# Gate and branch products turned to tokens-by-features in a two-layer encoder kernel, with the second half of the softmax scaling on ScalarE

## The chip, the cores and the metric

The kernel runs on one core of one Trainium2 chip. The metric is the device time of one execution, in microseconds (us). Before the change the median of three runs is 831.43 us (831.26 to 832.05).

## The reference, cut to what matters

256 tokens of width 1024 go through two layers. Everything is float32.

```python
h = rms_norm(x, norm1_g[l])
q, k, v ... = split(h @ w_in[l])            # four mixers A, B, C, D, four heads each
o_n = softmax(q k^T * scale + ...) v        # n = A..D, 256 columns each
y = einsum('bsnc,ncd->bsnd', o, w_branch[l])          # (256 x 256) @ (256 x 1024) per mixer
g = sigmoid(h @ w_gate[l] + b_gate[l])                # 256 x 4096
x = x + sum_n(g_n * y_n) @ w_o[l]
x = x + square(relu(rms_norm(x, norm2_g[l]) @ w_ff1[l])) @ w_ff2[l]
```

## The kernel before, in words

**Products.** Each weight is cut into a high part (`w_hi`, written by ScalarE, L575) and a low part (`w_lo`, raw minus high, written by VectorE, L810), each activation likewise (`act_hi`/`act_lo`, `part_hi`/`part_lo`). `split_product` (L1184 to L1193) makes one product out of three TensorE matmuls: high*high, high*low, low*high.

**Chunks.** The weights come in chunks of 1 MB or so, in the order of `CHUNKS`: 8 chunks of `w_in`, 16 of `w_gate` with the branch chunks `y` 0, 1, 2 between them, `y` 3, 4 of `w_o`, then `w_ff1` and `w_ff2` in turn. SyncE loads them in two halves into a raw ring of 2; the split parts live in a ring of 4. A chunk is split three steps before its product; ScalarE waits with it until the chunk four places earlier has been used (`w_used`). One step of the outer loop is one chunk; there are 28 steps before the `w_o` sums, and each engine walks through the same steps in its own hand-written order. The work of the four mixers (turning q and k, scores, softmax, turning the probabilities, values) is spread over these steps as `SCORES`, `SOFTMAX`, `TURN`, `VALUES`, `HEAD_OUT` and `X_AT` say; a pair of heads enters every second step. The softmax steps are the odd ones from 9 to 23.

**Gate and branch before.** A gate step takes 256 gate columns: two blocks of 128 features by 256 tokens, each 24 matmuls with the weight standing in the array and 256 tokens moving (`feature_blocks`, L1387 to L1390). ScalarE takes the result out of PSUM with the bias per partition (L696). A branch step makes four quarters of two feature blocks (`branch`, L1397 on); VectorE multiplies each by its gate (L1019, L1023) and adds it to `mix` (L1026). The branch results of the four mixers alternate between the two banks of `bank_w`, as do the gates; a product waits until the job two places earlier has been read (`bank_free`). After `y` 3, `mix` is cut into high and low parts (L748, L1005) and the `w_o` sums begin (`w_o_sums`).

**Softmax before.** VectorE finds the maxima (`maxima`), ScalarE takes the exponentials with their sums (L664), VectorE forms the reciprocals (L985) and scales both token tiles (L987), TensorE turns them (L1298).

**Order within a step before.** ScalarE: `heads_hi`, `probT_evac`, `evac((s,0))`, `exps`, `in_evac`, `split_hi` of chunk s+3, the gate of this step, `evac((s,1))`. VectorE: `maxima`, `heads_lo`, the first two quarters of a branch, `split_lo`, `normalise`, the last two quarters. TensorE: small product (s,0), chunk product, small product (s,1), scores, turned probabilities, values.

Of the kernel before, what the change touches and what calls it, by code (L numbers as in the profile page):

```python
# [18 lines left out]
ALU = mybir.AluOpType  # L19
# [3 lines left out]
P = 128  # L23
D = 1024
SEQ = 256
T = SEQ // P
# [26 lines left out]
Y_AFTER = {3 * n + 6: n for n in range(NB - 1)}  # L53
# [22 lines left out]
for _i in range(GATE_N):  # L76
    W_JOBS.append(("gate", _i, 0))
    if _i in Y_AFTER:
        W_JOBS += [("y", Y_AFTER[_i], q) for q in range(4)]
# [21 lines left out]
def pairs_at(first, s):  # L101
# [18 lines left out]
G1, G2, BG, GQ, GKV = 0, KD, 2 * KD, 2 * KD + NB * KD, 2 * KD + NB * KD + 2  # L120
NCOL = GKV + 1
VECTORS = {G1: KD, G2: KD, BG: NB * KD, GQ: 1, GQ + 1: 1, GKV: 1}
# [62 lines left out]
def trunk_kernel(nc, x, norm1_g, w_in, w_gate, b_gate, a_q_norm_g, a_k_norm_g, b_rel_bias, c_sink,  # L185
# [3 lines left out]
    with ctx:  # L189
# [44 lines left out]
        vec_all = sb("vec_all", [P, DEPTH * NCOL])  # L234
        root_row = sb("root_row", [P, SEQ])
# [35 lines left out]
        first_u = [bank_w[:, 0, 0:SEQ], bank_o[:, 0:SEQ]]  # L271
        turn_banks = [bank_o[:, :], bank_x[:, :], bank_acc[:, 0, :], bank_acc[:, 1, :]]
# [42 lines left out]
        x_evac = sem("x_evac")  # L315
        gate_tanh = sem("gate_tanh")
        scored = sem("scored")
        top_ready = sem("top_ready")
        exp_ready = sem("exp_ready")
        prob_ready = sem("prob_ready")  # L320
        prob_turned = sem("prob_turned")
# [6 lines left out]
        mixed = sem("mixed")  # L328
        mix_hi_ready = sem("mix_hi_ready")
# [35 lines left out]
        def split_view(buf, c):  # L365
            return buf[:, c % RING, 0:chunk_cols(c)]

# [38 lines left out]
        def _(sp):  # L406
# [3 lines left out]
            def load_half(c, h, l, g=0):  # L410
# [6 lines left out]
                if kind in ("in", "gate", "f1"):  # L417
                    w, n = {"in": (w_in, IN_C), "gate": (w_gate, 256), "f1": (w_ff1, 256)}[kind]
# [41 lines left out]
        def _(pool):  # L460
# [38 lines left out]

            def bias_run(l, r):  # L500
# [7 lines left out]
            for l in range(DEPTH):  # L508
                norm(2 * l, l)
                uq = d_w_uq[bass.ds(l, 1)].rearrange("o k n -> (o k) n")  # L510
# [35 lines left out]

                norm(2 * l + 1, l)
# [6 lines left out]
        def _(act):  # L554
# [112 lines left out]

            def probT_evac(i, l):
# [48 lines left out]
            for l in range(DEPTH):  # L717
# [11 lines left out]
                for s in range(STEPS):  # L729
# [16 lines left out]
                for q in range(4):  # L746
                    act.wait_ge(mixed, l * 12 + (8 + q + 1))
                    nc.scalar.activation(act_hi[:, 2 * q:2 * q + 2, :].rearrange("p k s -> p (k s)"), mix[:, q, :],  # L748
                                         ACT.Copy, scale=0.5).then_inc(mix_hi_ready, 1)
                split_hi(POS["o", 3], l)  # L750
                k = 2 * l + 1
# [36 lines left out]
        def _(dve):  # L788
# [190 lines left out]
            def normalise(i, l):  # L979
# [5 lines left out]
                chained(nc.vector.reciprocal(rsum[:, b, :], psum_p[:, b, :]), l)  # L985
# [15 lines left out]
            def mix_lo(q, l):  # L1001

                dve.wait_ge(mix_hi_ready, l * 4 + (q + 1))
                v = [a[:, 2 * q:2 * q + 2, :].rearrange("p k s -> p (k s)") for a in (act_hi, act_lo)]
                nc.vector.scalar_tensor_tensor(out=v[1], in0=mix[:, q, :], scalar=0.5, in1=f32(v[0]), op0=ALU.mult,  # L1005
                                               op1=ALU.subtract).then_inc(mix_lo_ready, 1)

            def branch(n, l, quarters):

                dve.wait_ge(gate_tanh, l * GATE_N + (4 * n + 4))  # L1010
                for q in quarters:
# [5 lines left out]
                    g = big[:, (4 * n + q) % 8, :]  # L1017
# [37 lines left out]
            for a, b, by in ((0, BG, 1.0), (BG, GQ, 0.5), (GQ, NCOL, 1.0)):  # L1055
                cols = slice(DEPTH * a, DEPTH * b)
                ins = nc.vector.tensor_scalar(vec_all[:, cols], bank_acc[:, 2, cols], by, None, ALU.mult)
            ins.then_inc(vec_ready, 1)
# [509 lines left out]
```

## Time and profile before

| | |
|---|---|
| median of 3 runs | 831.43 us |
| the profiled execution | 832.6 us, of which the span of the trace is 830.8 us |
| TensorE busy | 816.9 us (98%) |
| VectorE busy | 544.4 us (66%) |
| ScalarE busy | 409.6 us (49%) |
| GpSimd busy | 45.7 us (5%) |
| granted TensorE clock | 0.999 of full speed |
| DMA | 141.09 MB, mean 170 GB/s |

The busy times overlap: a core's engines run at the same time and wait for one another only through semaphores. "L1190" is line 1190 of the kernel. A row of the chain of waits gives start, length and what ran then on the path that ended last; a row of a timeline gives start, length, engine, line, operation, output<-inputs and shapes, and in brackets the idle time before it with the instruction that ended it.

### The profile page before, as it was taken

Reading aid. Unit: us, or ns where it says so; the run is one execution under the profiler, and the core shown is the slowest. Engines: PE = TensorE matmul, PEld = TensorE weight load, DVE = VectorE, ACT = ScalarE, POOL = GpSimd, SP = SyncE. Lnnn points to the kernel's source line nnn. Section 1 sums busy time; section 2 is a strip of 40 time slices with the busy share of each in tenths; the row PEclk is TensorE's granted clock in tenths of the full one; section 3 lists DMA queues with packets and bytes.
Section 4 is the critical chain, followed back from the end, with each engine's and each line's share of the span. In section 5 each row is a group of like instructions: output and inputs, shape, how many; then the busy total and the mean of one; then the engine's idle time right before and its main releaser. Section 6 shows DMA issues by size and latency. Waiting matters only on the chain.

```text
span 830.8 us, 14799 instructions
## 1 busy us (share of the span) xinstructions
PE 816.9 (98%) x5763; PEld 749.1 (90%) x5763; DVE 544.4 (66%) x805; ACT 409.6 (49%) x698; POOL 45.7 (5%) x81
## 2 busy tenths in 40 slices
PE   7999999999999999999999999999999999999996
PEld 6999979999899999999899999799988999999995
DVE  6687676865776665555767675687665865555663
ACT  6356655655454444333464475575545544333442
POOL 1420000000010000000013100000000100000000
PEclk9999999999999999999999999999999999999999
DMA  8976534536347555566546755334353665566541
GB/s 248 227 233 198 158 120 135 150 105 204 101 156 237 169 174 178 200 202 199 170 128 194 241 167 177 116 102 153 126 177 104 212 199 178 197 202 198 170 137 50
DMA packets 100851, 141.09 MB, mean 170 GB/s; under 512 B 4797, under 2 KB 87041, under 8 KB 100801
## 3 DMA queue, kind: packets, MB, share of 16 engines
q1 hardware_dynamic: 99296, 137.12, 52.1%
q0 software_dynamic: 1216, 3.17, 1.7%
q8 instruction: 34, 0.56, 0.3%
q14 instruction: 17, 0.13, 0.1%
q10 hardware_dynamic: 288, 0.11, 0.1%
HBM read 139.33 MB, written 1.05 MB: 169 GB/s over the span
## 4 chain that ended last, share of the span: by engine, by line
PE 93%; DVE 3%; ACT 1%; issue 1%; POOL 1%; DMA 1%; POOLq 0%; ACTq 0%; DVEq 0%
PE bank_w L1190 20%; PE bank_w L1192 19%; PE bank_w L1191 19%; PE bank_acc L1190 8%; PE bank_acc L1191 8%; PE bank_acc L1192 8%; PE bank_acc L1286 2%; PE bank_o L1315 2%; PE bank_acc L1298 2%; DVE w_lo L810 2%; DMA cst<-in_table 1%; PE bank_x L1263 0%; PE bank_x L1268 0%; POOL rstd L498 0%; PE bank_x L1259 0%
## 5 line engine op out<-in xcount | busy, mean ns | idle before, releaser
L810 DVE TENSOR_TENSOR w_lo<-raw,w_hi 128x1024 fp32r<-128x1024 f32 (+1 forms) x256 | 309.0, 1255 | 49.6 <-ACT w_hi L575 49.5
L1190 PE MATMUL bank_w<-act_hi,w_hi 128*128 128x256 f32 x1008 | 287.9, 286 | 0.0
L1192 PE MATMUL bank_w<-act_hi,w_lo 128*128 128x256 f32 x1008 | 285.8, 283 | 0.0
L1191 PE MATMUL bank_w<-act_lo,w_hi 128*128 128x256 f32 x1008 | 285.2, 283 | 0.0
L575 ACT ACTIVATE w_hi<-raw 128x1024 fp32r<-128x1024 f32 (+1 forms) x256 | 257.0, 1060 | 26.7 <-DMA raw<-in_w_gate 12.9
L1190 PEld LDWEIGHTS bank_w<-act_hi,w_hi 128*128 128x128 f32 x1008 | 191.6, 190 | 6.9 <-ACT big L696 3.5
L1191 PEld LDWEIGHTS bank_w<-act_lo,w_hi 128*128 128x128 f32 x1008 | 190.9, 189 | 1.8 <-issue 0.5
L1192 PEld LDWEIGHTS bank_w<-act_hi,w_lo 128*128 128x128 f32 x1008 | 191.2, 190 | 0.0
L704 ACT ACTIVATE part_hi<-big 128x512 fp32r<-128x512 f32 x32 | 20.3, 633 | 194.2 <-DVE big L1038 191.5
L1190 PE MATMUL bank_acc<-w_hi,part_hi 128*128 128x512 f32 x256 | 100.3, 392 | 0.0
L1191 PE MATMUL bank_acc<-w_lo,part_hi 128*128 128x512 f32 x256 | 100.3, 392 | 0.0
L1192 PE MATMUL bank_acc<-w_hi,part_lo 128*128 128x512 f32 x256 | 99.8, 390 | 0.0
L1038 DVE SCALAR_TENSOR_TENSOR big<-bank_w,root_row 128x512 f32<-128x512 f32 x30 | 20.7, 691 | 117.6 <-PE bank_w L1192 117.6
L1190 PE MATMUL bank_w<-w_hi,act_hi 128*128 128x268 f32 x256 | 73.9, 289 | 1.0 <-DVE act_lo L837 1.0
L1192 PE MATMUL bank_w<-w_hi,act_lo 128*128 128x268 f32 x256 | 73.2, 286 | 0.0
L1191 PE MATMUL bank_w<-w_lo,act_hi 128*128 128x268 f32 x256 | 73.2, 286 | 0.0
L696 ACT ACTIVATE big<-bank_w,vec_all 128x256 f32<-128x256 f32 x64 | 26.9, 473 | 66.0 <-PE bank_w L1192 66.0
L1192 PEld LDWEIGHTS bank_acc<-w_hi,part_lo 128*128 128x128 f32 x256 | 48.1, 188 | 10.6
L1190 PEld LDWEIGHTS bank_acc<-w_hi,part_hi 128*128 128x128 f32 x256 | 48.1, 188 | 9.5
L1191 PEld LDWEIGHTS bank_acc<-w_lo,part_hi 128*128 128x128 f32 x256 | 48.0, 188 | 8.9
L1190 PEld LDWEIGHTS bank_w<-w_hi,act_hi 128*128 128x128 f32 x256 | 48.1, 188 | 2.0 <-DVE w_lo L810 1.7
L1191 PEld LDWEIGHTS bank_w<-w_lo,act_hi 128*128 128x128 f32 x256 | 48.2, 188 | 0.0
(180 smaller groups left out, 938.5 us busy)
## 6 DMA issues: line engine op xcount, KB each, us to landing
raw<-in_w_ff SPq DMA_DIRECT2D x128, 512.0 KB, 4.7
raw<-in_w_gate SPq DMA_DIRECT2D x64, 512.0 KB, 4.7
raw<-in_w_in SPq DMA_DIRECT2D x32, 536.0 KB, 5.5
raw<-in_w_o SPq DMA_DIRECT2D x16, 512.0 KB, 4.5
raw<-in_w_branch SPq DMA_DIRECT2D x16, 256.0 KB, 4.5
raw<-in_w_branch SPq DMA_DIRECT2D x8, 512.0 KB, 4.6
xs<-in_x SPq DMA_DIRECT2D x2, 512.0 KB, 4.6
out_y<-big SPq DMA_DIRECT2D x4, 256.0 KB, 2.1
```

What stands on the lines that cost most here:

```text
L575: nc.scalar.activation(half_view(w_hi, c, h), raw_half(c, h), ACT.Copy).then_inc(w_hi_ready, 1)
L696: ins = nc.scalar.activation(big[:, i % 8, d * SEQ:(d + 1) * SEQ], bank[:, d * SEQ:(d + 1) * SEQ], ACT.Tanh, bias=vec(BG + 2 * i + d, l), ...
L704: nc.scalar.activation(part_hi[:, b, :, :].rearrange("p k s -> p (k s)"), relu[b], ACT.Square).then_inc(u_hi_ready, 1)
L810: nc.vector.tensor_tensor(half_view(w_lo, c, hf), raw_half(c, hf), f32(half_view(w_hi, c, hf)), ALU.subtract).then_inc(w_lo_ready, 1)
L1038: ins = nc.vector.scalar_tensor_tensor(out=relu[b].rearrange("p (d s) -> p d s", d=2), in0=bank_w[:, b, :].rearrange("p (d s) -> p d s", d ...
L1190: nc.tensor.matmul(dst, s_hi, m_hi, start=first, stop=False)
L1191: nc.tensor.matmul(dst, s_hi, m_lo, start=False, stop=False)
L1192: ins = nc.tensor.matmul(dst, s_lo, m_hi, start=False, stop=last)
L1286: ins = nc.tensor.matmul(bank_acc[:, half, keys], q[:, t * P:(t + 1) * P], k, start=True, stop=True)
L1298: ins = nc.tensor.transpose(bank_acc[:, 2 + b, at:at + P], prob[:, b, t, kt * P:(kt + 1) * P], ident)
L1315: ins = nc.tensor.matmul(bank_o[half * HD:(half + 1) * HD, blk * SEQ:(blk + 1) * SEQ], v, probT[:, half, kt, :], start=(kt == 0), stop=(kt ...
```

## The change

The gate and branch products are turned round: 128 tokens of the activation stand in the array and 512 weight columns move. A gate chunk is now half of the contraction (four of eight blocks of 128) for 512 columns; two chunks make a pair. In the even step of a pair both chunks are multiplied for token tile 0, in the odd step for tile 1, so that the second chunk of a pair is wanted one step earlier, and the first one is given back half-way through the second step. The gate bias now lies along the free axis: GpSimd loads it, spread over the partitions, in eight 256 KB transfers per layer, VectorE adds it while it takes the bank out of PSUM (`gate_add`), and ScalarE takes the tanh from SBUF. A gate's `gate_add` and tanh belong to the step after its product. `mix` comes out tokens by features, so each of its quarters is turned by four transposes (`turn_mix`) before it is cut for the `w_o` sums. Branch 0 moves from step 15 to 16, branch 2 from 23 to 24. VectorE scales only the first token tile of the probabilities, ScalarE the second one. On ScalarE `evac((s,1))` of a softmax step now stands ahead of the weight split, on VectorE the first two quarters of a branch stand ahead of the maxima and the last two right behind `heads_lo`. Four small products move by half a step to a step.

```diff
-Y_AFTER = {3 * n + 6: n for n in range(NB - 1)}
+Y_AFTER = {7: 0, 9: 1, 13: 2}
...
-    "lq": (11, 1), "lkv": (12, 1), "uq0": (15, 0), "uq1": (15, 1), "ukv0": (16, 0), "ukv1": (16, 1),
-    "dq0": (18, 1), "dk0": (19, 0), "dq1": (19, 1), "dk1": (20, 0),
+    "lq": (11, 1), "lkv": (12, 1), "uq0": (15, 1), "uq1": (16, 0), "ukv0": (16, 1), "ukv1": (17, 0),
+    "dq0": (18, 1), "dk0": (19, 0), "dq1": (20, 1), "dk1": (21, 1),
...
@@ SyncE
+                if kind == "gate":
+                    k = KD // 2 * (i % 2) + 2 * h
+                    src = w_gate.rearrange("l (k p) (c n) -> l c p k n", p=P, n=512)[l, i // 2]
+                    sp.dma_start(dst.rearrange("p (k n) -> p k n", k=2), src[:, k:k + 2, :]).then_inc(done, 16)
...
@@ GpSimd
+            def gate_bias(l, g):
+
+                row = b_gate[bass.ds(l, 1), g * 512:(g + 1) * 512]
+                pool.dma_start(gate_row[:, g % 2, :], row.to_broadcast([P, 512])).then_inc(gate_row_landed[g % 2], 16)
...
                 norm(2 * l, l)
+                pool.wait_ge(gate_read, l * GATE_N)
+                for g in range(2):
+                    gate_bias(l, g)
...
+                for g in range(2, GROUPS):
+                    pool.wait_ge(gate_read, l * GATE_N + 2 * (g - 1))
+                    gate_bias(l, g)
                 norm(2 * l + 1, l)
...
@@ ScalarE
-            for v, at, n in ((norm1_g, G1, KD), (norm2_g, G2, KD), (b_gate, BG, NB * KD)):
+            for v, at, n in ((norm1_g, G1, KD), (norm2_g, G2, KD)):
...
+            def normalise_second(i, l):
+
+                b = i % 2
+                act.wait_ge(rsum_ready, l * NH + (i + 1))
+                nc.scalar.activation(prob[:, b, 1, :], prob[:, b, 1, :], ACT.Copy,
+                                     scale=rsum[:, b, 1:2]).then_inc(prob_second_ready, 1)
...
-                act.wait_ge(w_used, used_count(l, POS["gate", i]))
-                if i >= 8:
-                    act.wait_ge(y_read, l * 16 + (i - 7))
-                bank = bank_w[:, W_AT["gate", i, 0] % 2, :]
-                for d in range(2):
-                    ins = nc.scalar.activation(big[:, i % 8, d * SEQ:(d + 1) * SEQ], bank[:, d * SEQ:(d + 1) * SEQ],
-                                               ACT.Tanh, bias=vec(BG + 2 * i + d, l), scale=0.5)
-                ins.then_inc(gate_tanh, 1)
+                g, t = divmod(i, 2)
+                z = gate_slot(g // 2, 2 * t + g % 2)
+                act.wait_ge(gate_read, l * GATE_N + (i + 1))
+                nc.scalar.activation(z, z, ACT.Tanh, scale=0.5).then_inc(gate_tanh, 1)
+
+            def mix_hi(q, l):
+
+                t, m = divmod(q, 2)
+                kcs = slice(m * KD // 2, (m + 1) * KD // 2)
+                act.wait_ge(mix_turned, l * 4 + (q + 1))
+                nc.scalar.activation(act_hi[:, kcs, t * P:(t + 1) * P], mix_banks[q].rearrange("p (k s) -> p k s", s=P),
+                                     ACT.Copy, scale=0.5).then_inc(mix_hi_ready, 1)
...
+                    if pair_heads(SOFTMAX, s):
+                        evac((s, 1), l)
                     for c in SPLIT_AT[s]:
                         split_hi(c, l)
-                    if kind == "gate":
-                        gate(j, l)
-                    evac((s, 1), l)
...
+                    if s > IN_N and CHUNKS[s - 1][0] == "gate":
+                        gate(CHUNKS[s - 1][1], l)
+                    if not pair_heads(SOFTMAX, s):
+                        evac((s, 1), l)
+                    for i in pair_heads(SOFTMAX, s):
+                        normalise_second(i, l)
+
+                mix_hi(0, l)
+                mix_hi(1, l)
                 split_hi(POS["o", 3], l)
+                mix_hi(2, l)
+                mix_hi(3, l)
...
@@ VectorE
-                for t in range(T):
-                    ins = nc.vector.tensor_scalar(prob[:, b, t, :], prob[:, b, t, :], rsum[:, b, t:t + 1], None, ALU.mult)
-                ins.then_inc(prob_ready, 1)
+                if i >= 2:
+                    dve.wait_ge(prob_second_ready, l * NH + (i - 1))
+                nc.vector.reciprocal(rsum[:, b, :], psum_p[:, b, :]).then_inc(rsum_ready, 1)
+                dve.wait_ge(rsum_ready, l * NH + (i + 1))
+                nc.vector.tensor_scalar(prob[:, b, 0, :], prob[:, b, 0, :], rsum[:, b, 0:1], None,
+                                        ALU.mult).then_inc(prob_ready, 1)
...
+            def gate_add(i, l):
+
+                g, t = divmod(i, 2)
+                if t == 0:
+                    dve.wait_ge(gate_row_landed[g % 2], 16 * (l * GROUPS // 2 + g // 2 + 1))
+                    dve.wait_ge(gate_first, l * GROUPS + (g + 1))
+                else:
+                    dve.wait_ge(w_used, used_count(l, POS["gate", i]))
+                nc.vector.tensor_tensor(gate_slot(g // 2, 2 * t + g % 2), bank_w[:, t, :], gate_row[:, g % 2, :],
+                                        ALU.add).then_inc(gate_read, 1)
...
+                    if s > IN_N and CHUNKS[s - 1][0] == "gate":
+                        gate_add(CHUNKS[s - 1][1], l)
+                    if kind == "y" and j < NB - 1:
+                        branch(j, l, (0, 1))
                     for i in pair_heads(SOFTMAX, s):
                         maxima(i, l)
                     for i in pair_heads(HEAD_OUT, s):
                         heads_lo(i, l)
                     if kind == "y" and j < NB - 1:
-                        branch(j, l, (0, 1))
+                        branch(j, l, (2, 3))
...
-                branch(NB - 1, l, (0,))
-                split_lo_half(POS["o", 2], 0, l)
-                branch(NB - 1, l, (1,))
+                branch(NB - 1, l, (0, 1, 2))
                 mix_lo(0, l)
-                split_lo_half(POS["o", 2], 1, l)
-                branch(NB - 1, l, (2,))
+                branch(NB - 1, l, (3,))
                 mix_lo(1, l)
-                branch(NB - 1, l, (3,))
+                split_lo(POS["o", 2], l)
+                split_lo(POS["o", 3], l)
                 mix_lo(2, l)
                 mix_lo(3, l)
-                split_lo(POS["o", 3], l)
...
@@ TensorE
+                pe.wait_ge(prob_second_ready, l * NH + (i + 1))
...
+                g, t = divmod(i, 2)
+                tok = slice(t * P, (t + 1) * P)
+                bank_free(("gate", g, t), l)
+                for half in range(2):
+                    c = POS["gate", 2 * g + half]
+                    hi, lo = k_view(w_hi, c, KD // 2), k_view(w_lo, c, KD // 2)
+                    if t == 0:
+                        pe.wait_ge(w_lo_ready, lo_count(l, c))
+                    sides = [(act_hi[:, half * KD // 2 + k, tok], act_lo[:, half * KD // 2 + k, tok], hi[:, k, :], lo[:, k, :])
+                             for k in range(KD // 2)]
+                    ins = split_product(bank_w[:, t, :], sides, half == 0, half == 1)
+                    if t == 1:
+                        ins.then_inc(w_used, 1)
...
+            def turn_mix(q, l):
+
+                pe.wait_ge(mixed, l * 12 + (8 + q + 1))
+                for j in range(KD // 2):
+                    ins = nc.tensor.transpose(mix_banks[q][:, j * P:(j + 1) * P], mix[:, q, j * P:(j + 1) * P], ident)
+                ins.then_inc(mix_turned, 1)
+
+            def last_branch(l):
+
+                for q in range(3):
+                    branch_part(NB - 1, q, l)
+                turn_mix(0, l)
+                branch_part(NB - 1, 3, l)
+                turn_mix(1, l)
...
                 for c in range(4):
-                    pe.wait_ge(mix_lo_ready, l * 4 + (c + 1))
+                    pe.wait_ge(mix_lo_ready, l * 4 + (c // 2 + 1))
...
+                    if c == 0:
+                        turn_mix(2, l)
+                        turn_mix(3, l)
+                pe.wait_ge(mix_lo_ready, l * 4 + 4)
                 part(0, 2)
```

## Rows read from the trace of the kernel before

**Rows 1.** The page: span, and busy time of each engine.
```profile
span 830.8 us, 14799 instructions
...
PE 816.9 (98%) x5763; PEld 749.1 (90%) x5763; DVE 544.4 (66%) x805; ACT 409.6 (49%) x698; POOL 45.7 (5%) x81
```

**Rows 2.** Busy time in one stretch: PE, PEld, DVE, ACT, POOL, clock, DMA.
```profile
60.00:190.00 130.00, 130.00 (x1030) 118.38 (x1029) 92.29 (x177) 78.29 (x168) 1.46 (x3) 1.00 0.47 142
```

**Rows 3.** Chain of waits around one gate product: start, us, what.
```profile
482.06 0.12 PE bank_w L1190
...
487.81 0.22 PE bank_x L1251 x2
```

**Rows 4.** Chain of waits in the MLP: 24 wide matmuls between these two.
```profile
327.22 0.24 PE bank_acc L1190
...
332.71 0.12 PE bank_w L1190
```

**Rows 5.** Groups of instructions: count, busy us, mean ns, idle before.
```profile
L810 DVE TENSOR_TENSOR w_lo<-raw,w_hi 128x1024 fp32r<-128x1024 f32 x224 | 262.2, 1219 | 48.9 <-ACT w_hi L575 48.9
...
L704 ACT ACTIVATE part_hi<-big 128x512 fp32r<-128x512 f32 x32 | 20.3, 633 | 194.2 <-DVE big L1038 191.5 <-DVE big L1035 2.7
...
L987 DVE TENSOR_SCALAR prob<-prob,rsum 128x256 f32<-128x256 f32 x64 | 19.7, 351 | 1.1
...
L1026 DVE TENSOR_TENSOR mix<-mix,tmp 128x512 f32<-128x512 f32 x24 | 16.6, 692 | 0.8
```

**Rows 6.** VectorE's timeline, steps 7 to 9 of layer 0, then step 8 of layer 1.
```profile
61.03 4.62 DVE L810 TENSOR_TENSOR w_lo<-raw,w_hi 128x1024 fp32r<-128x1024 f32 x4
...
71.50 0.48 DVE L908 COPY vd<-qkv 128x256 f32<-128x256 f32 x2
...
73.55 0.68 DVE L969 TENSOR_REDUCE top<-bank_acc 128x2 f32<-128x512 f32 x1
...
81.11 0.94 DVE L926 TENSOR_SCALAR qkv<-qkv,rs_d 128x192 f32<-128x192 f32 x4
...
478.45 0.49 DVE L908 COPY vd<-qkv 128x256 f32<-128x256 f32 x2
```

**Rows 7.** Chain of waits: layer 0's turning, small products, values; layer 1's turning.
```profile
60.63 0.44 PE bank_x L1247 x4
...
81.69 1.02 PE bank_acc L1298 x8
...
112.85 0.65 PE bank_x L1258 x2
113.50 0.84 PE bank_x L1259 x2
...
121.71 1.01 PE bank_o L1315 x8
...
468.04 0.44 PE bank_x L1247 x4
```

**Rows 8.** VectorE's timeline, layer 0, branch step 19.
```profile
146.67 0.70 DVE L967 SCALAR_TENSOR_TENSOR bank_acc<-cst,bank_acc 128x512 f32<-128x512 f32 x1 [0.90 <-PE bank_acc L1286]
...
149.73 0.69 DVE L1023 SCALAR_TENSOR_TENSOR tmp<-big,bank_w 128x512 f32<-128x512 f32 x1
```

**Rows 9.** ScalarE's timeline behind the last gate of layer 0.
```profile
205.73 0.84 ACT L696 ACTIVATE big<-bank_w,vec_all 128x256 f32<-128x256 f32 x2 [3.64 <-PE bank_w L1192]
206.46 2.01 ACT L575 ACTIVATE w_hi<-raw 128x1024 fp32r<-128x1024 f32 x2
```

**Rows 10.** Chain of waits, layer 0: the first transposes for the second norm.
```profile
226.13 0.22 PE bank_o L1201 x2
```

**Rows 11.** DMA issues: count, KB each, median us to landing.
```profile
raw<-in_w_gate SPq DMA_DIRECT2D x64, 512.0 KB, 4.7
...
w_ukv<-in_d_w_ukv POOLq DMA_DIRECT2D x2, 256.0 KB, 5.0
```

**Rows 12.** Chain of waits at the start of the kernel.
```profile
9.85 0.29 DVE vec_all L1057 x2
```

More of the change, by code:

```diff
@@ L75 @@
 W_JOBS = []
[L76 to L79, printed above, removed]
+for _g in range(GROUPS):
+    W_JOBS += [("gate", _g, t) for t in range(T)]
+    if 2 * _g + 1 in Y_AFTER:
+        W_JOBS += [("y", Y_AFTER[2 * _g + 1], q) for q in range(4)]
 W_JOBS += [("y", NB - 1, q) for q in range(4)]
@@ L315, in trunk_kernel @@
         x_evac = sem("x_evac")
+        gate_row_landed = [sem(f"gate_row_landed{b}") for b in range(2)]
+        gate_first = sem("gate_first")
+        gate_read = sem("gate_read")
         gate_tanh = sem("gate_tanh")
@@ L366, in split_view, with gate_slot @@
             return buf[:, c % RING, 0:chunk_cols(c)]
+        def gate_slot(n, q):
+            return big[:, (4 * n + q) % 8, :]
         def loads_of_half(c):
@@ L416, in load_half @@
                 dst = raw_half(c, h)
-                if kind in ("in", "gate", "f1"):
-                    w, n = {"in": (w_in, IN_C), "gate": (w_gate, 256), "f1": (w_ff1, 256)}[kind]
+                if kind == "gate":
+                    k = KD // 2 * (i % 2) + 2 * h
+                    src = w_gate.rearrange("l (k p) (c n) -> l c p k n", p=P, n=512)[l, i // 2]
+                    sp.dma_start(dst.rearrange("p (k n) -> p k n", k=2), src[:, k:k + 2, :]).then_inc(done, 16)
+                elif kind in ("in", "f1"):
+                    w, n = {"in": (w_in, IN_C), "f1": (w_ff1, 256)}[kind]
                     src = w.rearrange("l (k p) (c n) -> l c p k n", p=P, n=n)[bass.ds(l, 1), bass.ds(i + 2 * g, 1)]
@@ L1001, in mix_lo @@
             def mix_lo(q, l):
+                t, m = divmod(q, 2)
                 dve.wait_ge(mix_hi_ready, l * 4 + (q + 1))
-                v = [a[:, 2 * q:2 * q + 2, :].rearrange("p k s -> p (k s)") for a in (act_hi, act_lo)]
-                nc.vector.scalar_tensor_tensor(out=v[1], in0=mix[:, q, :], scalar=0.5, in1=f32(v[0]), op0=ALU.mult,
-                                               op1=ALU.subtract).then_inc(mix_lo_ready, 1)
+                hi, lo = (a[:, m * KD // 2:(m + 1) * KD // 2, t * P:(t + 1) * P] for a in (act_hi, act_lo))
+                nc.vector.scalar_tensor_tensor(out=lo, in0=mix_banks[q].rearrange("p (k s) -> p k s", s=P), scalar=0.5,
+                                               in1=f32(hi), op0=ALU.mult, op1=ALU.subtract).then_inc(mix_lo_ready, 1)
+            def gate_add(i, l):
[7 more added lines that the diff above has]
+                                        ALU.add).then_inc(gate_read, 1)
             def branch(n, l, quarters):
@@ L1054, in _ @@
             dve.wait_ge(rows_turned, 1)
[L1055 to L1058, printed above, removed]
+            nc.vector.tensor_copy(vec_all[:, :], bank_acc[:, 2, 0:DEPTH * NCOL]).then_inc(vec_ready, 1)
             dve.wait_ge(vec_ready, 1)
@@ L1091, in _ @@
                     if kind == "y" and j < NB - 1:
-                        branch(j, l, (2, 3))
                         for c in SPLIT_AT[s]:
@@ L1392, in gate @@
             def gate(i, l):
-                bank_free(("gate", i, 0), l)
-                pe.wait_ge(w_lo_ready, lo_count(l, POS["gate", i]))
-                feature_blocks(bank_w[:, W_AT["gate", i, 0] % 2, :], POS["gate", i])
+                g, t = divmod(i, 2)
[11 more added lines that the diff above has]
+                        ins.then_inc(w_used, 1)
@@ new lines, in gate, with branch_part @@
+                if t == 0:
+                    ins.then_inc(gate_first, 1)
+            def branch_part(n, q, l):
+                c, (t, m) = POS["y", n], divmod(q, 2)
+                tok, cols = slice(t * P, (t + 1) * P), slice(m * 512, (m + 1) * 512)
+                hi, lo = k_view(w_hi, c, 2), k_view(w_lo, c, 2)
+                if q == 0:
+                    pe.wait_ge(w_lo_ready, lo_count(l, c))
+                    pe.wait_ge(o_lo_ready, l * (NH // 2) + (2 * n + 2))
+                bank_free(("y", n, q), l)
+                sides = [(part_hi[:, n % 2, k, tok], part_lo[:, n % 2, k, tok], hi[:, k, cols], lo[:, k, cols]) for k in range(2)]
+                split_product(bank_w[:, W_AT["y", n, q] % 2, :], sides, True, True).then_inc(y_done if q < 3 else w_used, 1)
@@ L1397, in branch @@
             def branch(n, l):
-                c = POS["y", n]
-                pe.wait_ge(w_lo_ready, lo_count(l, c))
-                pe.wait_ge(o_lo_ready, l * (NH // 2) + (2 * n + 2))
-                hi, lo = k_view(w_hi, c, 2), k_view(w_lo, c, 2)
                 for q in range(4):
-                    bank_free(("y", n, q), l)
-                    for d in range(2):
-                        f = slice((2 * q + d) * P, (2 * q + d + 1) * P)
-                        sides = [(hi[:, k, f], lo[:, k, f], part_hi[:, n % 2, k, :], part_lo[:, n % 2, k, :]) for k in range(2)]
-                        ins = split_product(bank_w[:, W_AT["y", n, q] % 2, d * SEQ:(d + 1) * SEQ], sides, True, True)
-                    ins.then_inc(y_done if q < 3 else w_used, 1)
+                    branch_part(n, q, l)
@@ L1525, in _ @@
                         gate(j, l)
-                    if kind == "y":
+                    if kind == "y" and j < NB - 1:
                         branch(j, l)
@@ L1534, in _ @@
                         values(j2, l)
+                last_branch(l)
                 w_o_sums(l)
```

21 lines of the change are left out of this document (11 added, 10 removed).

## The prediction

> **What bounds the kernel now.** I read the page first. TensorE is busy for 816.9 of 830.8 us [rows 1], so almost nothing but its own work sets the time. The stretch with the gates and the mixers confirms it: in 130 us TensorE is busy for 130.00, VectorE for 92.29 (71%), ScalarE for 78.29 (60%) [rows 2]. So the change can gain only by making TensorE's work shorter, and it loses wherever TensorE, which hardly waits today, has to wait for an engine that has got later. Then I read the chain of waits for what one product costs, and the timelines of VectorE and ScalarE for when each bank, weight and gate is ready.
>
> **Wider matmuls.** One gate product today is 48 matmuls with 256 moving columns: from 482.06 to 487.81, 5.75 us, or 120 ns each [rows 3]. The MLP's second product is what the new form looks like, 24 matmuls with 512 moving columns: from 327.22 to 332.71, 5.49 us, or 229 ns each [rows 4]. The arithmetic is the same, so a step gains 0.26 us. Other steps in the trace lie a little lower than 5.75, and I take 0.25. There are 16 gate steps and 3 branch steps per layer (branch 3 is costed with the tail), 38 in all: **minus 9.5 us**. Bounds: 0.15 a step (5.7) to 0.32 (12.2). The Trainium skill (TensorE: Matmul & The Clock Gate, Back-to-back issue gap) gives a matmul its columns at the full clock plus only some 2.5 ns; making one matmul of each of 960 pairs would then give back about 2.4 us. The rows say 240 against 229 ns per 512 columns, and I go by them.
>
> **Startup.** Three small instructions behind the turned vectors (two seen in 0.29 us on the chain [rows 12]) become one: minus 0.2.
>
> **VectorE and ScalarE in total.** VectorE gains 16 adds of 0.69 us per layer and gives away 16 scalings of 0.35 [rows 5]: plus 5.4 us in some 130, 75% busy instead of 71%. ScalarE trades two tanh instructions for one of some 0.63 (as the 512-wide one [rows 5]) and takes the scalings: about even. In the sum this is free, hidden under TensorE. What costs is order: a gate's add now stands at the front of VectorE's next step, behind everything of the step before, and the product two jobs later waits for it.
>
> **Steps 9 to 11.** VectorE ends its step 8 at 73.55 [rows 6]; the new add puts the maxima at 74.25. From there to `d_norm` it took 7.56 us (to 81.11), and 0.94 for `d_norm` [rows 6]. ScalarE now copies `cq` ahead of the split (plus 0.5), VectorE saves two scalings (minus 0.5), so gate 1's add ends at 74.25 + 7.56 + 0.94 + 0.7 = 83.4. Gate 3's product uses the same bank. Today it starts when the turning ends, 81.69 + 1.02 = 82.7 [rows 7]; three gates at 0.25 less make that 82.0. Wait: 1.4. In layer 1 TensorE is 407.41 us later (60.63 to 468.04 [rows 7]), VectorE only 406.95 (71.50 to 478.45 [rows 6]): 0.9. **Plus 2.3** (0 if VectorE's start is earlier by as much; 4).
>
> **Steps 15 and 16, branch 0.** The copy of `uq0` is asked of ScalarE ahead of the split of chunk 18, but TensorE makes `uq0` only behind gate 7. From gate 7's start: product 5.5, `uq0` 1.5 (0.65 + 0.84 [rows 7]), ScalarE's copy 0.65, both high parts 2.0 [rows 9], the last low part 1.3 (1.22 and a hand-over [rows 5]), the reciprocals and first scalings of two heads 1.0, gate 7's add 0.7: 12.65. TensorE meanwhile does product 5.5, `uq0` 1.5, values 1.0 [rows 7], `uq1` 1.5, first quarter of branch 0 1.4: 10.9, and the second quarter needs the bank of gate 7. Wait 1.8, twice: **plus 3.6** (0 to 5).
>
> **Step 19, branch 1.** Today the maxima of two heads, 146.67 to 149.73, run before VectorE touches the branch [rows 8], at a time when TensorE is still on other work. Now VectorE first waits for the first quarter: from the start of branch 1, 1.6; two quarters of multiply and add, 2.7, to 4.3; maxima 3.1, to 7.4; multiply of the third quarter, to 8.1. TensorE ends the branch at 5.5 and the values at 6.5, and gate 10 needs that bank. Wait 1.6, twice: **plus 3.2** (1 to 4.5). Branch 2 meets no maxima; gate 13's add comes 0.2 late by the same count: **plus 0.4**.
>
> **The tail, branch 3 to the second norm.** Today from 205.6, where gate 15's product ends, to 226.13: 20.5 us [rows 9, 10]. Afterwards, counted from that same end: ScalarE splits chunk 30 first (2.0 [rows 9]) and only then does the last tanh, to 2.85; VectorE multiplies quarter 0 to 3.6, which frees the bank; TensorE has done quarters 0 and 1 by 2.9 and now does quarter 2 (3.65 to 5.05), turns quarter 0 (0.44 [rows 7], 5.5), quarter 3 (6.9), turns quarter 1 (7.35). VectorE goes through add 0, quarters 1 and 2 and reaches the low part of quarter 0 at 7.6. The `w_o` sums start at 7.7 and hold 60 wide matmuls, 13.75, four transposes twice, 0.9, and 0.35 for hand-overs: 22.7. The splits of chunks 30 and 31 end at about 12.5 and 15, before their sums. **Plus 2.2 per layer, 4.4** (3 to 6); the 32 transposes alone are 3.5 of it.
>
> **At nothing.** The second chunk of a pair is wanted one step earlier. Tightest is chunk 9 in layer 0: low parts done at about 63.4 (four from 61.03 [rows 6]), wanted half-way through gate 0 at 61.07 + 2.75 = 63.8; if that cover goes, it costs what is missing, tenths. SyncE issues no more loads, and `w_gate` comes in runs twice as long; 512 KB land in 4.7 us as before [rows 11]. GpSimd issues eight loads of 256 KB more per layer (`w_ukv`, of that size, lands in 5.0 us [rows 11]), each asked for at least two steps, 12 us, ahead of its use. Two of them run beside the first `w_in` chunks: 0, at worst 2 us once, as layer 0's seventh chunk has no slack. Scaling the second tile on ScalarE makes the turning wait for a second engine, which is inside the 2.3.
>
> **Sum.** 2.3 + 3.6 + 3.2 + 0.4 + 4.4 = 13.9, minus 9.5, minus 0.2: plus 4.2 us. The profiled execution took 832.6 (span 830.8 [rows 1]), so it would become 836.8; the median shown is 1.2 below that execution, and I forecast 835.6.
>
> **The rivals.**
> *The engines in time.* The waits at branches 0 and 1 (6.8) don't come about. Place: gate 7's add and the third quarter of branch 1. It decides from the point where VectorE is 1.8 us earlier there than I count, for example as the hand-overs overlap better. Speaking for it: VectorE is idle for a quarter of the stretch [rows 2]. Against: the idle time lies in front of ScalarE's high parts, and both waits follow from a fixed order. Then 835.6 - 6.8 = 828.8; with steps 9 to 11 in time as well, 826.5. Chance 0.2.
> *A draw.* Half of the waits, or the wide matmuls at the good end: 830 to 833. Chance 0.13.
> *More waits than I see.* The extra transfer delays layer 0's weights, or the later engines are late at a further bank: plus 2 to 5, 838 to 841. Chance 0.12.
> *Wide matmuls gain nothing.* The difference of 240 and 229 ns comes of what else the MLP does and not of the width, so that 48 narrow matmuls and 24 wide ones take the same in the gates: 835.6 + 9.5 = 845.1. For it speaks that I have no wide matmul beside the mixers' work; against it, that the `w_o` sums, with VectorE busy, are as fast as the MLP. Chance 0.03. By the formula cited from the Trainium skill it would be 842.7.
> My forecast, 833 to 838, keeps 0.52.
>
> **The numbers.** 835.6 us. The range is 828.0 to 840.0: it leaves out the best part of the first rival and the worst of the last two. About 0.2% (1.7 us) is what a measurement can tell from no change: faster by more than that 0.2, within 0.13, slower 0.67.
>
> **What would show it.** In the profile afterwards: 960 matmuls of 512 columns at 229 ns from start to start in the gates (right if a gate step takes 5.5); TensorE waiting for the add of the gate (two spots per layer, at branch 0 and gate 3) and for the multiply of a branch (gate 10) for 1 to 2 us each; the tail 22 to 23 us long. The forecast is wrong if TensorE's busy share stays at 98% and the span falls by the full 5, or if a gate step still takes 5.7.

## The result: 0.45% slower, and the profile after

The changed kernel takes 835.21 us (median of 5, 834.95 to 835.51) against 831.43 us before (median of 5): plus 3.78 us, ratio 1.0045 with a 95% interval of 1.0030 to 1.0059. Run again later beside other kernels it took 835.07 against 832.23: plus 2.84, ratio 1.0033 (1.0020 to 1.0045). "The changed kernel" below stands about 3.3 us above the kernel before. The page of the profile after begins so; line numbers are those of the changed kernel:

```profile
span 833.4 us, 12968 instructions
...
PE 814.8 (98%) x4835; PEld 700.5 (84%) x4835; DVE 550.4 (66%) x803; ACT 416.2 (50%) x698; POOL 55.7 (7%) x97
...
PE 87%; DVE 7%; ACT 2%; issue 1%; DMA 1%; POOL 1%; POOLq 0%; ACTq 0%; DVEq 0%
```

TensorE is busy 2.1 us less than in [rows 1], although it has 32 transposes more, and the span is 2.6 us longer: it waits. The last line is the chain that ended last. VectorE and ScalarE hold 9% of it, where they held 4% in the kernel before:

```profile
PE 93%; DVE 3%; ACT 1%; issue 1%; POOL 1%; DMA 1%; POOLq 0%; ACTq 0%; DVEq 0%
```

At a share of TensorE that still rounds to 98% this is the first sign that other engines now sit between TensorE's products. The stretch of [rows 2] says the same (columns as there), TensorE at 126.87 of 130 us where it had 130.00:

```profile
60.00:190.00 130.00, 126.87 (x624) 96.15 (x623) 92.94 (x170) 82.89 (x172) 4.72 (x9) 1.00 0.50 159
```

VectorE has 92.94 us in it where it had 92.29, but that is the stretch and not its work: from 12 to 200 us it has 138.09 where it had 134.07.

**A wide gate product**, from the chain of waits of layer 1 (start, us, what), between the turning ahead of it and the one behind it:

```profile
482.54 0.44 PE bank_x L1302 x4
482.98 0.23 PE bank_w L1245
...
488.53 0.22 PE bank_x L1306 x2
```

That is 5.55 us for 24 matmuls, 231 ns each, against 5.75 in [rows 3].

**Who held TensorE up**, from the waits of TensorE's matmuls (for whom: us in total, times, longest):

```profile
PE bank_w L1245 <- DVE tmp L1081: 3.2, 4, 1.4
PE bank_w L1245 <- DVE big L1063: 2.9, 3, 1.2
```

L1063 is the new add of the gate, L1081 the multiply of a branch with its gate. In the kernel before there was no such add, and the multiply (L1023 there) held TensorE up for 0.9 us, in two waits. The chain shows the places. Branch 0, second quarter, layer 0:

```profile
119.41 1.06 ACT w_hi L603
120.48 0.98 DVE w_lo L854
121.63 1.22 DVE w_lo L854
...
123.68 0.69 DVE big L1063
124.42 0.50 PE bank_w L1245
```

ScalarE begins the split of chunk 18 only at 119.41, right behind its copy of `uq0` (asked for first, and made by TensorE only behind gate 7). VectorE's low parts follow, then the scalings, then the add, and TensorE starts at 124.42. Branch 1 and gate 10:

```profile
152.05 0.62 DVE bank_acc L1011
152.69 0.70 DVE top L1013
153.58 0.62 DVE bank_acc L1011
154.22 0.70 DVE top L1013
155.02 0.70 DVE tmp L1081
155.76 0.50 PE bank_w L1245
```

The four rows of the maxima stand between the second and the third quarter of the branch, and gate 10 starts when the third has been multiplied. And the tail, of which [rows 9, 10] showed the old form:

```profile
206.39 1.04 ACT w_hi L603
207.44 0.53 ACT big L729
207.99 0.70 DVE tmp L1081
...
212.05 0.61 DVE act_lo L1052
...
212.71 0.50 PE bank_acc L1245
...
215.74 0.87 PE bank_acc L1487 x8
...
228.12 0.44 PE bank_acc L1256 x4
```

The last tanh waits behind a split; from 207.99 to 212.67 VectorE alone is on the path; the first two turnings (in `bank_o` and `bank_x`) are not on it; only the last two, the eight transposes at 215.74, are.

**Where the 2.6 us of span come from**, by the same event in both traces:

| event | before | after | shift |
|---|---|---|---|
| first product | 11.98 | 11.31 | -0.67 |
| ScalarE released by gate 15, layer 0 | 205.73 | 205.43 | -0.30 |
| second norm's last four transposes, layer 0 | 226.57 | 228.12 | +1.55 |
| turning behind the `w_in` step 7, layer 1 | 468.04 | 469.25 | +1.21 |
| ScalarE released by gate 15, layer 1 | 613.13 | 613.88 | +0.75 |
| second norm's last four transposes, layer 1 | 633.99 | 636.57 | +2.58 |

The gates and mixers about break even, as the wide products pay for the waits. The two tails cost 1.85 and 1.83 us. Between the first tail and layer 1's gates 0.34 us comes back, and behind the second tail nothing changes: the span is 2.6 us longer.

### The profile page after: what moved, and what is told of

Same layout as the page of the kernel before. It is cut to its first block, busy times and chain, and to the rows that moved or that the text cites. A ratio compares the mean times of both kernels' runs of the same rounds, so it can differ in the third digit from the quotient of the medians.

```text
span 833.4 us, 12968 instructions
## 1 busy us (share of the span) xinstructions
PE 814.8 (98%) x4835; PEld 700.5 (84%) x4835; DVE 550.4 (66%) x803; ACT 416.2 (50%) x698; POOL 55.7 (7%) x97
## 4 chain that ended last, share of the span: by engine, by line
PE 87%; DVE 7%; ACT 2%; issue 1%; DMA 1%; POOL 1%; POOLq 0%; ACTq 0%; DVEq 0%
PE bank_w L1245 18%; PE bank_w L1247 18%; PE bank_w L1246 18%; PE bank_acc L1245 8%; PE bank_acc L1246 8%; PE bank_acc L1247 8%; DVE w_lo L854 3%; PE bank_acc L1341 2%; PE bank_acc L1354 2%; PE bank_o L1371 1%; DVE tmp L1081 1%; ACT w_hi L603 1%; DVE mix L1084 1%; DMA raw<-in_w_gate 1%; DMA cst<-in_table 0%
## 5 line engine op out<-in xcount | busy, mean ns | idle before, releaser
L1245 PE MATMUL bank_w<-w_hi,act_hi 128*128 128x268 f32 (+1 forms) x512 | 178.1, 348 | 4.0 <-DVE tmp L1081 2.7
L1247 PE MATMUL bank_w<-w_hi,act_lo 128*128 128x268 f32 (+1 forms) x512 | 173.9, 340 | 0.0
L1246 PE MATMUL bank_w<-w_lo,act_hi 128*128 128x268 f32 (+1 forms) x512 | 173.7, 339 | 0.0
L1247 PE MATMUL bank_w<-act_hi,w_lo 128*128 128x256 f32 x496 | 141.2, 285 | 0.0
L1246 PE MATMUL bank_w<-act_lo,w_hi 128*128 128x256 f32 x496 | 140.8, 284 | 0.0
L1245 PE MATMUL bank_w<-act_hi,w_hi 128*128 128x256 f32 x496 | 139.8, 282 | 0.0
L1247 PEld LDWEIGHTS bank_w<-w_hi,act_lo 128*128 128x128 f32 x512 | 96.2, 188 | 11.0
L1245 PEld LDWEIGHTS bank_w<-act_hi,w_hi 128*128 128x128 f32 x496 | 94.1, 190 | 1.2
L1246 PEld LDWEIGHTS bank_w<-act_lo,w_hi 128*128 128x128 f32 x496 | 93.4, 188 | 1.3
L1247 PEld LDWEIGHTS bank_w<-act_hi,w_lo 128*128 128x128 f32 x496 | 93.8, 189 | 0.0
```

What stands on the lines that cost most here:

```text
L1245: nc.tensor.matmul(dst, s_hi, m_hi, start=first, stop=False)
L1246: nc.tensor.matmul(dst, s_hi, m_lo, start=False, stop=False)
L1247: ins = nc.tensor.matmul(dst, s_lo, m_hi, start=False, stop=last)
```

## The experiments

Each expectation was written before its run. Every run was compared with the kernel before on the same chip: that had 832.25 us beside the first four kernels, 832.26 beside the second four, 832.23 beside the last four.

### One order taken back

```diff
 e1: ScalarE
-                    if pair_heads(SOFTMAX, s):
-                        evac((s, 1), l)
                     for c in SPLIT_AT[s]:
                         split_hi(c, l)
                     if s > IN_N and CHUNKS[s - 1][0] == "gate":
                         gate(CHUNKS[s - 1][1], l)
-                    if not pair_heads(SOFTMAX, s):
-                        evac((s, 1), l)
+                    evac((s, 1), l)
 e2: VectorE
-                    if kind == "y" and j < NB - 1:
-                        branch(j, l, (0, 1))
                     for i in pair_heads(SOFTMAX, s):
                         maxima(i, l)
+                    if kind == "y" and j < NB - 1:
+                        branch(j, l, (0, 1))
```

> The changed kernel (835.2) with ScalarE's evac((s,1)) of the softmax steps back behind the weight split and the tanh; nothing else. Theory of the fixed order: the wait at the second quarter of branch 0 (1.8 us in each layer) goes, as ScalarE no longer sits idle until TensorE has made uq0: 835.2 - 3.6 = 831.6, and the row of TensorE waiting for the add of gate 7 is gone. Rival (VectorE is late there because it has more to do in all, not because of the order): within 0.5 of 835.2.

> The changed kernel (835.2) with the maxima back ahead of the first two quarters of a branch on VectorE; nothing else. Theory of the fixed order: gate 10 no longer waits 1.6 us for the multiply of the third quarter of branch 1, in each layer: 835.2 - 3.2 = 832.0. Rival (the maxima only change places with the wait, so that quarter 2 of branch 1 waits instead): within 0.5 of 835.2.

Measured: e1 831.62 us, ratio 0.9991 (0.9981 to 1.0000); e2 832.57, ratio 1.0003 (0.9993 to 1.0013). Against the changed kernel at 3.3 above, that is minus 3.9 and minus 3.0 for 3.6 and 3.2 forecast. The rivals, within 0.5 us of the changed kernel, are out. In the waits of e1's matmuls the add is gone and the multiply is what it was:

```profile
PE bank_w L1242 <- DVE tmp L1078: 3.2, 4, 1.4
```

and in e2 it is the other way round, the multiply is down to tenths:

```profile
PE bank_w L1245 <- DVE big L1063: 3.2, 4, 1.2
...
PE bank_w L1245 <- DVE tmp L1081: 0.5, 2, 0.3
```

So the wait of gate 10 comes of the order that e2 takes back, the wait at branch 0 of the order that e1 takes back, and neither comes back elsewhere when it is taken away alone.

Not all of e1's 3.9 us is branch 0, though. From the scores of the fourth pair to those of the fifth, with branch 0 between them, the changed kernel takes 19.80 us (109.86 to 129.66) and e1 18.35: 1.45 a layer, 2.9 in all. The rest may be gate 3, whose wait is gone in e1's profile as well. But that wait is not the same in every execution: the second profile of the changed kernel, r_after, hardly has it (the scores of the second pair to those of the third take 15.23 us, against 16.01 in the first profile and 15.04 in e8 below), because ScalarE could split the second half of chunk 11 at 67.27 and not at 68.23. Its span is 833.4 us like the first one's. So e1 does not pin the wait of gate 3 to an order.

### The width

```diff
 e3: TensorE, gates; the branch quarters likewise
-                for half in range(2):
+                for w, half in ((0, 0), (0, 1), (1, 0), (1, 1)):
...
-                    ins = split_product(bank_w[:, t, :], sides, half == 0, half == 1)
-                    if t == 1:
+                    ins = split_product(bank_w[:, t, cols], sides, half == 0, half == 1)
+                    if t == 1 and w == 1:
```

Here `cols` is the half w of the 512 columns, of the moving operand as well.

> The changed kernel (835.2) with every wide product of the gates and branches made as two column halves of 256, each through the whole contraction: 1920 matmuls of 256 columns for 960 of 512. Theory (a wide matmul saves 10 to 11 ns against two narrow ones): 0.25 us a step, 10 in all with branch 3; steps 9 to 11 hide up to 1.5 of it, and chunk 9 is wanted 1.4 us earlier: 843 to 845, a gate step 5.7 us or more. Rival (the width saves a few ns a matmul): 836 to 838. Rival (nothing): 835.

Measured: 847.53 us, ratio 1.0185 (1.0168 to 1.0202), 12.0 above the changed kernel and more than any theory had. The waits say why:

```profile
PE bank_w L1245 <- DVE big L1063: 6.9, 6, 1.3
...
PE bank_w L1245 <- DVE tmp L1081: 2.6, 2, 1.3
PE bank_w L1245 <- DVE w_lo L854: 1.9, 2, 0.9
```

They add up to 5 us more than the changed kernel's 3.2 and 2.9. The form gives a pair's first chunk back three quarters through the odd step instead of half-way, so ScalarE splits later and VectorE adds later: ScalarE's splits waited 17.1 us for TensorE here and 9.1 in the changed kernel. It also wants a pair's second chunk a quarter through the even step and not half-way, and the 1.9 us of waits for low parts can come of either; no run separates the two. About 7 us are left by subtraction for the width and for what the waits list does not hold. The expectation had priced the width, and the early want of chunk 9, and forgotten the release.

### The softmax part

```diff
 e4, on the kernel before; e5 is the reverse, on the changed kernel
+            def normalise_second(i, l):
+
+                b = i % 2
+                act.wait_ge(rsum_ready, l * NH + (i + 1))
+                nc.scalar.activation(prob[:, b, 1, :], prob[:, b, 1, :], ACT.Copy,
+                                     scale=rsum[:, b, 1:2]).then_inc(prob_second_ready, 1)
```

> The kernel before (831.4) with the softmax part of the change alone: ScalarE scales the second token tile of the probabilities, VectorE the first. My theory: TensorE turns the probabilities a microsecond or more after both are ready in most steps, so no change: 831.2 to 832.2. Rival (the turning now waits for ScalarE, whose scaling stands behind the tanh and a copy that wait for TensorE): 1 us or more slower, 832.5 to 836, with TensorE waiting for the scaled tile.

> The changed kernel (about 3.8 us above the kernel before) with its softmax part taken back: VectorE scales both token tiles of the probabilities, ScalarE none. Theory (the waits at gate 3 and at branch 0 stand behind VectorE's scalings): VectorE is 0.5 us later at each of them: 1 to 2 us slower than the changed kernel, 4.8 to 5.8 above the kernel before. Rival (the scalings cost nothing on either engine, as in the kernel before): 3.8 above. Second rival (ScalarE's share delays the turning): 1 us or more faster than the changed kernel.

Measured: e4 832.17 us, ratio 0.9999 (0.9990 to 1.0009), no change, as expected. e5 837.85, ratio 1.0063 (1.0048 to 1.0079), 5.6 above the kernel before and 2.3 above the changed one. The same edit is worth nothing where TensorE does not wait for VectorE and some 2 us where it does, since the scalings stand ahead of the add for which TensorE waits. In e5 that wait is 5.1 us in six waits, where the changed kernel has 2.9 in three, and the one for the multiply is unchanged:

```profile
PE bank_w L1241 <- DVE big L1059: 5.1, 6, 1.7
```

ScalarE needs longer for it, 508 ns on average where VectorE's scaling takes 354, and no wait of TensorE's matmuls for ScalarE's scaling shows in the changed kernel.

### The tail

```diff
 e6: ScalarE, last step
+                    if s == STEPS - 1:
+                        gate(CHUNKS[s - 1][1], l)
                     for c in SPLIT_AT[s]:
                         split_hi(c, l)
 e7: TensorE; mix_hi and mix_lo then read mix instead of the turned banks
-                for j in range(KD // 2):
-                    ins = nc.tensor.transpose(mix_banks[q][:, j * P:(j + 1) * P], mix[:, q, j * P:(j + 1) * P], ident)
-                ins.then_inc(mix_turned, 1)
```

In e7 the `w_o` sums get untransposed values, so it tells of time alone.

> The changed kernel with ScalarE doing the tanh of gate 15 ahead of the high parts of chunk 30 in the last step; nothing else. Theory (the tail hangs on ScalarE's order first, then on VectorE): VectorE begins branch 3 at 207.4 instead of 208.0 in layer 0's place, 0.6 us per layer: 1.2 us below the changed kernel, 2.6 above the kernel before. Rival (TensorE's own products and transposes bound the tail): no change, 3.8 above.

> The changed kernel without the 32 transposes of mix: the high and low parts are cut straight from mix, so that the w_o sums get the mixed values untransposed; everything else as it was. Theory (the first two turnings of a layer lie behind VectorE's branch work and cost nothing, the last two lie in TensorE's path): 2 x 0.87, so 1.7 us below the changed kernel, 2.1 above the kernel before. Rival (all 32 are in the path): 3.5 us below the changed kernel, 0.3 above the kernel before.

Measured: e6 834.25 us, ratio 1.0023 (1.0014 to 1.0033), 2.0 above the kernel before where 2.6 was expected and 3.8 by the rival. As the changed kernel itself came out at 3.8 and at 2.8, the times alone leave 0.8 to 1.8 us for the edit. The traces settle it. From the last product of the values to the norm's last four transposes on TensorE's timeline, layer 0, the changed kernel first and e6 second:

```profile
198.59 1.08 PE L1371 MATMUL bank_o<-probT,vd 128*64 128x256 f32 x8
227.96 0.60 PE L1256 MATMUL bank_acc<-cst,xs 128*128 128x128 f32 x4
```

```profile
197.79 1.08 PE L1373 MATMUL bank_o<-probT,vd 128*64 128x256 f32 x8
226.61 0.60 PE L1258 MATMUL bank_acc<-cst,xs 128*128 128x128 f32 x4
```

29.37 us against 28.82, and the same in layer 1 and in the changed kernel's second profile. That is 0.55 a layer for 0.6 expected, and the rival is out.

e7 takes 833.08 us, ratio 1.0009 (1.0000 to 1.0019), 0.8 above it. With the changed kernel at 2.8 to 3.8, the transposes come to 2.0 to 3.0 by the times, between 1.7 (theory) and 3.5 (rival). The trace decides: from the start of the `w_o` sums to the last four transposes of the norm layer 0 takes 15.41 us in the changed kernel (212.71 to 228.12) and in e7

```profile
212.39 0.47 PE bank_acc L1245
226.85 0.44 PE bank_acc L1256 x4
```

14.46, so 0.95 less; and from gate 15's end to the start of the sums nothing is saved (205.45 to 212.71 there, 205.08 to 212.39 here). The theory holds: in each layer half of the transposes are free.

### All orders together, and three variations of it

```diff
 e8: e1, e2 and e6 together, and on VectorE
                         gate_add(CHUNKS[s - 1][1], l)
+                    if s == 10:
+                        d_norm(l)
...
-                    if s == 9:
-                        d_norm(l)
 e9: e8 with the edit of e3. e10: e8 with the edit of e5. e11: e8 with the edit of e7
```

> The changed kernel with four orders mended together: ScalarE's copy behind the split, the maxima ahead of a branch, d_norm behind gate 1's add, the last tanh ahead of the split. Theory (the waits are separate and each comes from its own order): minus 4.4, minus 3.5, minus 0.5, minus 1.2 against the changed kernel: 5.8 below the kernel before, 826.4 where that has 832.2. Rival (a wait taken away comes back at the next bank): half of it, 828 to 830.

Measured: 827.42 us, ratio 0.9942 (0.9928 to 0.9956): 4.8 below the kernel before, and the fastest here that computes the whole. The four edits are worth 8.1 us together (9.6 expected); half of it, the rival, is out. The three orders that were also run alone come to 3.9, 3.0 and 1.3, 8.2 in sum. The fourth, `d_norm` behind the add, was not run alone, and nothing is left for it in the times: what it is worth is not shown. Of TensorE's waits for VectorE in the gates tenths are left:

```profile
PE bank_w L1244 <- DVE act_lo L880: 0.8, 1, 0.8
PE bank_o L1255 <- DVE big L860: 0.4, 1, 0.4
PE bank_w L1244 <- DVE w_lo L853: 0.3, 1, 0.3
```

> The changed kernel once more, unchanged, beside the next three on one chip, so that their differences have a base: 3.8 us above the kernel before (2.5 to 4.9).

Measured: plus 2.84, within the interval expected.

> The kernel with the four mended orders (4.8 us below the kernel before), with every wide product made as two halves of 256 columns. TensorE waits for almost nothing there, so the difference is the worth of the width. From the traces of before and after (0.17 us a step between landmarks, 40 steps with branch 3): plus 7, and up to 1.5 more for chunk 9 wanted 1.4 us earlier: 834.5 to 836 where the kernel before has 832.3. By the prediction's 0.25 a step: plus 10, with chunk 9 11, so 837.5 to 838.5. Rival (a few ns a matmul): plus 2 to 3, 830.

Measured: 843.82 us, ratio 1.0137 (1.0121 to 1.0152), 16.4 above e8: outside all three. The late release again. ScalarE's splits waited for TensorE 8.3 us in e8 and 25.8 in e9, as the waits of ScalarE say, e8's first:

```profile
ACT w_hi L603 <- PE bank_w L1246: 8.3, 8, 2.6
```

```profile
ACT w_hi L603 <- PE bank_w L1246: 25.8, 14, 4.1
```

and TensorE's matmuls for VectorE 4.6 us for the add, 1.9 for low parts, 1.1 for the multiply. So this run does not price the width by its time. It does between landmarks where TensorE does not wait: from the scores of the second pair to those of the third, two gate steps, layer 0, e8 first and e9 second:

```profile
79.52 1.06 PE bank_acc L1340 x8
...
94.56 1.06 PE bank_acc L1340 x8
```

```profile
81.55 1.06 PE bank_acc L1340 x8
...
96.92 1.06 PE bank_acc L1340 x8
```

15.04 against 15.37 us, 0.165 a step, and the next pair nearly the same (14.40 against 14.71). The kernel before, with narrow products of the other orientation, had 15.39 and 14.74: so in these intervals it is the width that pays, and turning the product round pays nothing by itself. Over 38 steps that is 6.3 us. The waits above are 7.3 more than e8's. That leaves 2.8 of e9's 16.4. A part may be that the first matmul behind a wait takes longer on the chain than one in a row (0.38 against 0.12 us in e9), which the waits list does not count; how much of the 2.8 it is, is not shown.

> The kernel with the four mended orders (4.8 us below the kernel before), with both scalings back on VectorE. Theory (the softmax part is worth something only where a wait hangs on VectorE): with those waits gone it is worth 0 to 0.5 us: 4.3 to 4.8 below the kernel before. Rival (it is worth 1.8 us as in the changed kernel): 3.0 below.

> The kernel with the four mended orders without the 32 transposes of mix (the w_o sums get untransposed values). Theory (with the last tanh early, the first two turnings of a layer lie in TensorE's path as well, as the chain of waits shows): 3.0 to 3.5 us less, 7.8 to 8.3 below the kernel before. Rival (only the two behind the first sum count, as in the changed kernel): 1.7 less, 6.5 below.

Both theories fell, and for one reason: each took the path that the trace showed and not the one just behind it. In both the rival came near.

e10: 829.60 us, ratio 0.9967 (0.9954 to 0.9980), 2.6 below the kernel before (3.0 by the rival, 4.3 to 4.8 by the theory) and 2.2 worse than e8, so the scalings cost about what they cost in the changed kernel. In layer 0 TensorE loses 0.54 us against e8 around branch 1 (8.67 us from the scores to the values behind them, against 8.13) and 0.49 around branch 2 (7.10 from the values to the next turning, against 6.61); twice the two is 2.1. The chain of e10 shows branch 2 waiting behind the scalings, at a place where e8 has no wait:

```profile
183.94 0.62 DVE prob L1028 x2
184.56 0.61 DVE big L1058
...
185.21 0.50 PE bank_w L1240
```

e11: 825.66 us, ratio 0.9920 (0.9905 to 0.9935), 1.8 better than e8 and not 3.0 to 3.5; the rival had said 1.7. In e8 the chain went over the turnings of the first two quarters (207.90 below), but VectorE's low part, on its own timeline, ended at the same time:

```profile
207.90 0.44 PE bank_x L1486 x4
208.38 0.50 PE bank_acc L1244
```

```profile
207.64 0.68 DVE L1051 SCALAR_TENSOR_TENSOR act_lo<-bank_o,act_hi 128x512 fp32r<-128x512 f32 x1
```

TensorE was through at 208.34 and VectorE at 208.32. Taking TensorE's part away leaves VectorE's, and the sums start when they did: 13.58 us behind the last product of the values in e8 and 13.62 in e11. A chain names the last of two; it does not say how far behind the other is.

## Why the prediction was right, point by point

The forecast was 835.6 us, the kernel takes 835.2. The sign and the mechanism hold: wide products pay, and a fixed order on two engines and the tail take more back. That it came within 0.4 us is luck in good part. The forecast was plus 4.2; the first comparison gave plus 3.8, the second 2.8, and the traces 2.6. The sizes were off in both directions and cancelled in part, by the landmarks of the traces:

| term | forecast | measured |
|---|---|---|
| wide matmuls, 38 steps | -9.5 | -6.4 |
| steps 9 to 11 | +2.3 | +1.0 |
| branch 0 | +3.6 | +2.9 |
| branch 1 | +3.2 | +2.8 |
| branch 2 | +0.4 | about 0 |
| tail | +4.4 | +3.7 |
| start | -0.2 | -0.7 |
| `w_in` phase of layer 1 | 0 | -0.3 |
| sum | +4.2 | +3.0 (the span: +2.6) |

**Wide matmuls.** The term that was mis-sized most. I took 0.25 us a step from one gate product of 5.75 and the MLP's 5.49. In the gates a wide product takes 5.55, and between landmarks a step gains 0.155 to 0.175. Why a wide matmul is 2 ns slower there than in the MLP is not shown. It lies in the range that I gave (0.15 to 0.32) but at its low end. The rival by which the width gains nothing, and the 2.4 us of the formula of the Trainium skill (TensorE: Matmul & The Clock Gate, Back-to-back issue gap), which the page gives for an isolated matmul, are both out: 6.4 us. By that formula a wide matmul takes 216 ns; here it takes 231.

**Start.** 0.43 of the 0.67 us is there before anything that the change touches on this chain: the first transposes of the norm start at 7.21 and not at 7.64, as `x` had landed sooner, which no run ties to the change. The rest is the forecast 0.2.

**VectorE in total.** The prediction gave VectorE 75% of the stretch from 60 to 190 us, and the changed kernel shows 71%. The count was right for a kernel in which TensorE doesn't wait: e8 has 97.06 us of 130 there, 75%.

**Steps 9 to 11.** The place was right in layer 0. VectorE's timeline:

```profile
80.63 0.94 DVE L970 TENSOR_SCALAR qkv<-qkv,rs_d 128x192 f32<-128x192 f32 x4
81.48 0.68 DVE L1063 TENSOR_TENSOR big<-bank_w,gate_row 128x512 f32<-128x512 f32 x1
```

Gate 3 starts at 82.22, where TensorE could have at about 81.4: 0.8 instead of 1.4, and 1.0 by the scores on either side (16.01 us against e8's 15.04). In layer 1 it doesn't wait, where 0.9 was forecast. The step that failed is that VectorE ends its step 8 as late as before: ScalarE took the last high part of chunk 11 at 68.23 instead of 69.26, since that half landed sooner. In r_after it landed sooner still, and the wait was all but gone. So the 1.0 is that of one execution.

**Branches 0 and 1.** At branch 0 the scores on either side are 1.45 us further apart than in e1, for 1.8 forecast. Gate 10 waited 1.4 for 1.6. e1 and e2 show the causes.

**The tail.** 1.85 us per layer for 2.2. That the last tanh stands behind the split was right (e6). I had put the 32 transposes down as 3.5 of the 4.4, and that was wrong: half of them lie beside VectorE's branch work, and e7 gives 0.95 us a layer for the rest. My own count had it so, with the second turning over at 7.35 and VectorE at the low part only at 7.6.

**The engines in time**, the rival at 0.2, would have needed VectorE 1.8 us earlier at two places. e8 shows that this is what mended orders bring. That its 827.4 is near the 826.5 to 828.8 that I gave it is chance in part: e8 also has a shorter tail, and the width gives back 3.1 us less than I counted.

**At nothing.** The gate rows (landed in 4.2 us, median), the second chunk a step earlier and the longer runs of `w_gate` cost nothing that the traces show, beyond 0.2 us of waiting for low parts in r_after. ScalarE's share of the scaling belongs here too: it is slower than I took it for, and the turning did not wait for it.

## What to carry to other kernels

When a product gets cheaper on an engine that never waits, list every buffer it hands over and put the reader's queue beside it: here 6.4 us of cheaper matmuls met 6.7 us of waits at three hand-overs and 3.7 us of longer tail, and putting orders right in two instruction lists gave back 8.1. A busy share doesn't show them (VectorE has 71% of the stretch with the gates before and after, and 75% in the kernel with the waits mended), the chain and a timeline of one step do. Price a matmul beside the work that will run with it, not in the quietest phase of the kernel, and before crediting the removal of something on the chain look how close the next path is.

## What the runs showed of the hardware

A matmul with 512 moving columns costs 229 ns in the MLP and 231 in the gates, two with 256 columns 240 in the kernel before and 238 in e9, at a granted clock of 1.00 throughout. In these products half as many matmuls of twice the width gave back 3% of the time. And scaling a 128x256 tile from and to SBUF takes ScalarE 508 ns and VectorE 354, though ScalarE's copy of 128x256 out of PSUM takes 385: I had reckoned with about the latter.
